# Index list and ranks of the expert selection in PSUM, and a dummy GELU behind an exponential, in a two-layer decoder trunk

## What is computed

```python
v1, i1 = lax.top_k(s1, PEER_TOPK)          # 16 of 128 keys, for each token and head
v2, i2 = lax.top_k(s2, PEER_TOPK)
cand = (v1[..., :, None] + v2[..., None, :]).reshape(PEER_BLOCK, PEER_HEADS, PEER_TOPK * PEER_TOPK)
top, ci = lax.top_k(cand, PEER_TOPK)
idx = jnp.take_along_axis(i1, ci // PEER_TOPK, axis=-1) * N_KEYS + jnp.take_along_axis(i2, ci % PEER_TOPK, axis=-1)
gate = jax.nn.softmax(top, axis=-1)
u_sel = expert_u[idx]
act = jax.nn.gelu(jnp.einsum('td,tkd->tk', xb, u_sel).astype(jnp.float32))
coeff = (gate * act).astype(xb.dtype)
return jnp.einsum('tk,tkd->td', coeff, expert_v[idx])
```

## Time and profile before

| | |
|---|---|
| median of three runs | 2200.14 us |
| profiled execution: time, span | 2200.17 us, 2198.4 us |
| PE busy | 2106.0 us, 96% |
| DVE busy | 1533.8 us, 70% |
| ACT busy | 985.8 us, 45% |
| POOL busy | 803.9 us, 37% |
| chain that ended last | PE 75%, DVE 15%, issue 7%, DMA 2% |
| mean granted clock of TensorE | 0.983 of full speed |

### The profile page before, as it was taken

One profiled execution on the slowest core, in us unless ns is written; L12 is line 12 of the kernel. 1 busy time (PEld: TensorE's weight loads), 2 busy tenths in 40 slices (PEclk: granted clock), 3 DMA queues, 4 the chain that ended last, 5 costly groups with the idle time before them and its releaser, 6 DMA issues.

```text
span 2198.4 us, 45771 instructions
## 1 busy us (share of the span) xinstructions
PE 2106.0 (96%) x14382; PEld 1957.3 (89%) x14382; DVE 1533.8 (70%) x3212; ACT 985.8 (45%) x1367; POOL 803.9 (37%) x322
## 2 busy tenths in 40 slices
PE   6799999999999999999988999998999999999997
PEld 5799799999998888899978998998999988888997
DVE  1543319998888888777735531599899788887776
ACT  2554444544543333344445444445545433333443
POOL 3488678910000000144354986698000000003442
PEclk8799999999999999999999999999999999999999
DMA  6345447654457777755453554576554587776553
GB/s 174 128 145 184 150 150 227 201 179 159 158 177 236 241 241 241 220 182 190 163 178 112 176 185 146 168 228 190 160 166 163 192 241 243 241 241 198 185 187 124
DMA packets 155042, 410.72 MB, mean 187 GB/s; under 512 B 17331, under 2 KB 67668, under 8 KB 154924
## 3 DMA queue, kind: packets, MB, share of 16 engines
q1 hardware_dynamic: 154220, 407.75, 57.7%
q0 software_dynamic: 704, 1.57, 0.6%
HBM read 382.00 MB, written 27.26 MB: 186 GB/s over the span
## 4 chain that ended last, share of the span: by engine, by line
PE 75%; DVE 15%; issue 7%; DMA 2%; ACT 0%; SPq 0%; DVEq 0%; ACTq 0%; POOLq 0%
PE bank L1043 36%; PE bank L1241 31%; PE bank L1293 5%; DMA rel_scratch<-act 2%; DVE area L921 2%; DVE area L924 2%; DVE area L881 2%; DVE area L901 1%; DVE area L878 1%; DVE area L793 1%; DVE area L898 1%; DVE area L926 1%; DVE area L885 1%; DMA ring<-in_stream 1%; DVE area L890 1%
## 5 line engine op out<-in xcount | busy, mean ns | idle before, releaser
L440 POOL TENSOR_TENSOR halves<-ring,halves 128x1024 fp32r<-128x1024 f32 x308 | 797.7, 2604 | 1357.6 <-ACT halves L505 1356.1
L1043 PE MATMUL bank<-hT,halves 128*128 128x256 f32 x8688 | 1125.8, 286 | 24.4 <-POOL halves L440 11.4
L505 ACT ACTIVATE halves<-ring 128x1024 fp32r<-128x1024 f32 x668 | 707.4, 1060 | 925.8 <-PE bank L1043 467.0
L1043 PEld LDWEIGHTS bank<-hT,halves 128*128 128x128 f32 x8688 | 1071.8, 192 | 34.6 <-issue 11.2
L1241 PE MATMUL bank<-halves,coef 128*128 128x512 f32 x3072 | 713.2, 391 | 3.9 <-DVE coef L977 3.9
L1241 PEld LDWEIGHTS bank<-halves,coef 128*128 128x128 f32 x3072 | 574.5, 189 | 123.0 <-DVE coef L977 5.9
L938 DVE TENSOR_TENSOR halves<-ring,halves 128x1024 fp32r<-128x1024 f32 x360 | 438.6, 1219 | 39.2 <-issue 22.1
L971 DVE TENSOR_TENSOR act<-act,area 128x256 f32<-128x256 f32 x256 | 223.7, 874 | 100.3 <-ACT act L615 95.4
L951 DVE TENSOR_SCALAR onehot<-ids,x 128x128 f32<-128x128 f32 x512 | 172.9, 338 | 1.9 <-issue 1.9
L1293 PE MATMUL bank<-onehot,x 128*128 128x128 f32 x1024 | 156.2, 274 | 0.0
L950 DVE TENSOR_SCALAR x<-ids,x 128x128 f32<-128x128 f32 x512 | 142.4, 278 | 18.2 <-PE bank L1293 17.1
(11 more groups left out here) (136 smaller groups left out, 973.0 us busy)
## 6 DMA issues: line engine op xcount, KB each, us to landing
ring<-in_stream SPq DMA_DIRECT2D x672, 512.0 KB, 3.5
held_blocks<-act SPq DMA_DIRECT2D x188, 128.0 KB, 1.9
act<-held_blocks SPq DMA_DIRECT2D x188, 128.0 KB, 3.1
area<-rel_scratch SPq DMA_DIRECT2D x2, 1024.0 KB, 6.6
rel_scratch<-act POOLq DMA_DIRECT2D x1, 1532.0 KB, 35.7
area<-in_consts SPq DMA_DIRECT2D x2, 576.0 KB, 3.8
x<-in_x SPq DMA_DIRECT2D x1, 1024.0 KB, 5.0
out_y<-x SPq DMA_DIRECT2D x2, 512.0 KB, 2.7
```

The costliest lines, as they stand in the source:

```text
L440: pool.tensor_tensor(halves[:, s, 1, :], ring[:, s, :], halves[:, s, 0, :].bitcast(F32), ALU.subtract)\
L505: a.activation(halves[:, s, 0, :], ring[:, s, :], ACT.Copy).then_inc(hi_done, 1)
L1043: i = pe.matmul(o, stationary[a], moving[b], start=begin and n == 0, stop=end and n == len(TERMS) - 1)
```

## The change

`idf`, the index list as floats (512 elements a partition), and the two ranks `caf` and `cbf` (256 each) lived in SBUF, as parts of `area`. Now `idf` is bank 4 of PSUM and the two ranks are the halves of bank 5. The casts L887, L917 and L918 write there, each comparison L921 reads its rank from there, and each product L924 reads its index list from there; each has its other input still in SBUF, and writes to SBUF. On ACT one activation with GELU on a single column is added directly behind the exponential.

```diff
-        idf = part(TT, PH, 2, TOPK)
...
-        caf = part(TT, PH, TOPK)
-        cbf = part(TT, PH, TOPK)
...
+        idf = bank[4][:, :].rearrange("p (t h c r) -> p t h c r", t=TT, h=PH, c=2)
+        caf, cbf = (bank[5][:, c * S:(c + 1) * S].rearrange("p (t h r) -> p t h r", t=TT, h=PH) for c in range(2))
...
                 a.wait_ge(shifted_ready, l + 1)
                 a.activation(sel[:, 2], sel[:, 2], ACT.Exp).then_inc(gexp_ready, 1)
+                a.activation(stat[:, 13:14], one, ACT.Gelu_apprx_tanh)
...
-                v.tensor_copy(caf, ca)
-                link(v.tensor_copy(cbf, cb))
+                v.tensor_copy(caf.rearrange("p t h r -> p (t h r)"), ca.rearrange("p t h r -> p (t h r)"))
+                link(v.tensor_copy(cbf.rearrange("p t h r -> p (t h r)"), cb.rearrange("p t h r -> p (t h r)")))
```

## The result

The changed kernel takes 2183.68 us (median of four runs, 2183.15 to 2184.57), against 2200.38 us before (four runs, 2198.88 to 2202.81). The ratio is 0.9925, with a 95% interval of 0.9912 to 0.9938: faster by 16.7 us, three quarters of a per cent. The profiled execution took 2183.15 us with a span of 2181.4 us.

The account below looks back on a forecast made before the run. PE was taken to wait beside the index lookup for ACT, POOL and DVE, late one after another. Reaching the transposes at 441.75 instead of 449.48 us saves 7.7 us a layer: 2200.2 - 15.4 = 2184.8 us, range 2182 to 2191.

Parts of the forecast that it names:

- The picture of turns: Index lookup: DVE instructions with two SBUF inputs and POOL's alternate, each waiting for the other's whole instruction; a round is 11.1 us.
- DVE's term: Lookup L921 and L924: 2.29 us each instead of 4.38; four rounds save 16.9 us, gates ready at 432.4 us.
- Rivals 1 and 3: Lookup on DVE: PSUM broadcast no faster, 2200 us, chance 0.05; or halfway at 3.83 us an instruction, 2190.8 us, 0.04.
- rival 2: Lookup on DVE: broadcast reads from PSUM cost more than 4.4 us; slower, 2205 us at 4.7 us an instruction, chance 0.03.
- POOL's term: Subtraction beside the lookup: back to 2.42 us, below PE's 2.86 for a block, so PE's three waits for POOL go.
- PE at the transposes: PE resumes behind the exponential at 418.8 us and reaches the transposes at 441.7, after the gates at 432.4.
- The dummy: Added GELU on ACT behind the exponential: worth about 2.3 us a layer in company, nearly nothing alone.
- Its first half: Behind the exponential, the dummy leaves 0.2 to 0.25 us of PE's 1.46 us wait: 1.2 us gained.
- Its second half: Second round of the loop: the dummy avoids table loads that would cost 1.1 us with POOL repaired.
- Rival 4: The dummy on ACT is dearer or fails its part: some 1.4 us a layer, 2187.6 us, chance 0.03.
- What was late next: Behind the transposes: DVE starts about 0.9 us later, 2 us are left before the one-hots, PE is the bound.
- The size: Up to the transposes: 449.48 - 441.75 = 7.7 us saved a layer, 15.4 us in two.

Follow-up runs that it names:

- e3: The changed kernel with the ranks back in SBUF, so only the index list in PSUM, dummy GELU kept: 2183.00 us, ratio 0.9925.
- e9: The kernel before plus the dummy GELU, with the sums L926 cut to the first of 16 terms: 2198.14 us, ratio 0.9999.
- e6: The changed kernel with each sum L926 done three times, so that the gates come later: 2199.36 us, ratio 1.0000.
- e1: The changed kernel without the dummy GELU: 2190.86 us, ratio 0.9963.
- e4: The changed kernel with the index list back in SBUF, so only the two ranks in PSUM, dummy GELU kept: 2184.32 us, ratio 0.9935.
- e2: The kernel before with the dummy GELU alone, index list and ranks still in SBUF: 2198.72 us, ratio 0.9997.
- e8: The changed kernel run again unaltered in a later group, as yardstick: 2185.84 us, ratio 0.9937.

## Why the prediction was right, step by step

**The picture of turns** held, and e3 shows it on one instruction: 4.4 us behind a subtraction under way, 2.29 where it comes into a gap, and then POOL's subtraction is the one that waits. The Trainium skill (SBUF — State Buffer, "Who interferes with whom") states that a DVE instruction with two SBUF inputs contends with GpSimd's reads and that a reduction never does. The traces agree: with two SBUF inputs L921 and L924 take 4.4 us, with one 2.29, and the reduction L926 takes 2.29 in both kernels.

**DVE's term.** Forecast 2.29 us an instruction, measured 2.291 and 2.286. The gates are ready at 430.77 against 432.4. Of these 1.6 us the earlier start of the layer is 0.7, and L932 is 1.3: I had kept 4.0 us for it, and it takes 2.70 where POOL is not always busy. The dearer casts take some of it back. Rivals 1 and 3 fall, since a broadcast from PSUM costs nothing extra here, and rival 2 with them.

**POOL's term.** Forecast 2.42 us and no waits; measured 2.41 (the mean from 400 to 440 us) and none. (The forecast calls PE's third wait for POOL, 1.25 us, like the one of 0.76; the sum does not use them singly.) The experiments add what the sum could not show, since it took both terms together: each of the two, POOL (e9) and the gates (e6), is enough to lose everything.

**PE at the transposes.** Forecast 441.7 us, measured 441.11 in a layer that began 0.7 us early.

**The dummy.** Its first half held: 0.2 us were to remain of PE's 1.46, and the window shows 0.13 us of idle time. Its second half was too small. I gave the dummy 2.3 us a layer in company; without it the two stalls are 1.46 and 1.40 us (I had 1.1 for the second; ACT's two loads, copy and GELU take 4.04 us from 428.48 where I had 3.9, and start some 0.2 us behind the block), and each adds some time in which PE starts and ends, so that from 413.8 us to the transposes e1 needs 30.38 us and the changed kernel 27.38: 3.0 us a layer. By medians e1 stands 7.9 us above e3 and 6.5 above e4 of its group, more than these 6.0; the difference stays open, within the spread between executions. The forecast of the whole did not depend on this split. Rival 4 falls too. The Trainium skill (ScalarE: Activation LUTs, "What ACT_TABLE_LOAD costs") has 2.66 us for each switch of table; the trace does not agree, since the dummy starts 1.30 us behind the start of its load.

**What was late next.** I had PE as the bound behind the transposes, with about 0.9 us less in hand at the one-hots; DVE's L938 starts 2.53 us behind the transposes instead of 1.70, and no wait stands before L1293. Right.

**The size.** 15.4 us forecast, 15.3 in the two stretches that it was about, 16.7 by the medians. What is beyond 15.4 is of the order of the spread between groups of runs, and no merit of the forecast: of the 17.0 us between the two traces 1.6 are the clock behind one wait, which comes out either way from one execution to the next.

## What to carry to other kernels

Where two engines are late by nearly the same amount, the chain that ended last names one of them, and relief of that one alone brings nothing (e9 and e6 brought 0.3 us and none); ask of a change whether it moves both. Here the two were late by one cause, DVE instructions with two SBUF inputs beside a steadily working GpSimd, and one operand in a free PSUM bank removed it; half the instructions were enough. Where a loop on the chip needs two functions and is entered with a third's table, look for table loads inside its body: one dummy activation of the loop's function ahead of it made them go here, where the loop's other function, a copy, needs no load behind it. It pays only if nothing else is late in their shadow (e2).

## What I had not expected of the hardware

- Waits cost PE more than their length when the granted clock falls behind them. Behind the wait of 6.0 us in e6 it is 0.72 over 8 us, in both layers (48 matmuls in 7.56 us instead of 5.99). Behind waits of 0.8 to 1.8 us in the kernel before it stayed at 1.00. Between these it goes either way: behind the wait of 1.9 us in the last stage (shown with the result), and behind a wait of 2.38 us the changed kernel needs 15.49 us for 60 matmuls in the first layer and 13.90 in the second, and e8, the same kernel, the other way round (13.90, then 15.32). So a single trace can carry 1.6 us at such a place that another execution does not have.
- A cast of 256 elements to PSUM takes 0.42 us (L918) where the one to SBUF took 0.29 us, and the copy L735 of 512 elements 0.69 from PSUM against 0.43 from SBUF in a gap of POOL: for this copy PSUM pays only beside a busy POOL.
- The ring of four slots covers a POOL whose mean is above PE's pace (2.98 against 2.87 us, e3) for 40 us without one wait.
